# Rotary rotation of q and k by ScalarE copies between partition halves, instead of a TensorE product with a rotation matrix

## What is computed

```python
z = rms_norm_2(x, norm_g) @ w_in
aq, ak, av, ag, mq, mk, mv, mi, mf, mo, mgate = split(z)
q = rms_norm_2(aq.reshape(B, L, 16, 64), q_norm_g)     # a norm per token and head
k = rms_norm_2(ak.reshape(B, L, 2, 64), k_norm_g)
# rope on the first 16 of a head's 64 rows, in two halves of 8
x1, x2 = x[..., :8], x[..., 8:16]
x = concat([x1 * cos - x2 * sin, x2 * cos + x1 * sin, x[..., 16:]])
ya = sliding_window_sink_attention(q, k, v, sink)      # window 128, meta tokens always seen
```

## Time and profile before

| | |
|---|---|
| runs | 1529.10, 1522.83, 1528.91 us, median 1528.91 |
| the profiled execution's own time | 1525.94 us |
| its span | 1524.0 us |
| TensorE busy | 1480.7 us, 97% |
| VectorE busy | 1052.0 us, 69% |
| ScalarE busy | 765.5 us, 50% |
| GpSimd busy | 318.6 us, 21% |
| mean granted TensorE clock | 0.994 |

### The profile page before, as it was taken

The page is one execution under the profiler, slowest core; times in us unless marked ns, Lnnn a source line. Parts: engine busy times, 40 slices in busy tenths (PEclk is TensorE's granted clock), DMA queues, the critical chain, the costliest instruction groups (busy, mean ns, idle before and its releaser), DMA issues.

```text
span 1524.0 us, 31453 instructions
## 1 busy us (share of the span) xinstructions
PE 1480.7 (97%) x11939; PEld 1460.6 (96%) x11939; DVE 1052.0 (69%) x1999; ACT 765.5 (50%) x1270; POOL 318.6 (21%) x392
## 2 busy tenths in 40 slices
PE   7999998999999999999999999999999999999998
PEld 7999998899999999999999999889999999899898
DVE  6666578766655666557766656888678778876883
ACT  5454448555444554445554545446644453565442
POOL 4111113211101111014321114453320125231000
PEclk9999999999999999999999999999999999999999
DMA  6656754465555655554565555533343554334333
GB/s 207 186 179 200 241 166 139 152 189 184 181 174 185 186 184 181 173 188 154 162 192 180 179 176 157 152 107 116 91 119 107 164 145 123 99 98 125 111 117 120
DMA packets 245275, 239.65 MB, mean 157 GB/s; under 512 B 15160, under 2 KB 244392, under 8 KB 245048
## 3 DMA queue, kind: packets, MB, share of 16 engines
q1 hardware_dynamic: 245176, 238.29, 50.9%
HBM read 237.21 MB, written 1.05 MB: 156 GB/s over the span
## 4 chain that ended last, share of the span: by engine, by line
PE 84%; DVE 10%; ACT 2%; issue 2%; POOL 1%; DMA 0%; SPq 0%; DVEq 0%; ACTq 0%; POOLq 0%
PE bank L552 25%; PE bank L554 25%; PE bank L553 25%; DVE w_lo L1523 3%; PE bank L878 1%; PE bank L818 1%; PE bank L836 1%; ACT w_hi L967 1%; PE bank L801 1%; DVE work L1563 1%; DVE work L1680 1%; PE bank L884 1%; PE bank L894 1%; PE bank L817 1%; PE bank L837 0%
## 5 line engine op out<-in xcount | busy, mean ns | idle before, releaser
L1523 DVE TENSOR_TENSOR w_lo<-raw,w_hi 128x1024 fp32r<-128x1024 f32 (+1 forms) x456 | 563.0, 1244 | 303.8 <-ACT w_hi L967 303.5
L552 PE MATMUL bank<-x_hi,w_hi 128*128 128x256 f32 (+1 forms) x2480 | 719.0, 290 | 2.2 <-DVE w_lo L1523 2.2
L554 PE MATMUL bank<-x_hi,w_lo 128*128 128x256 f32 (+1 forms) x2480 | 707.1, 285 | 0.0
L553 PE MATMUL bank<-x_lo,w_hi 128*128 128x256 f32 (+1 forms) x2480 | 706.2, 285 | 0.0
L967 ACT CAST w_hi<-raw 128x1024 fp32r<-128x1024 f32 (+1 forms) x456 | 464.9, 1030 | 261.2 <-PE bank L554 250.1
L552 PEld LDWEIGHTS bank<-x_hi,w_hi 128*128 128x128 f32 x2480 | 476.0, 192 | 4.1 <-issue 2.0
L553 PEld LDWEIGHTS bank<-x_lo,w_hi 128*128 128x128 f32 x2480 | 476.1, 192 | 1.0
L554 PEld LDWEIGHTS bank<-x_hi,w_lo 128*128 128x128 f32 x2480 | 475.6, 192 | 0.0
L552 PE MATMUL bank<-y_hi,w_hi 128*128 128x256 f32 (+1 forms) x1088 | 310.2, 285 | 8.0 <-DVE y_lo L1534 8.0
L554 PE MATMUL bank<-y_hi,w_lo 128*128 128x256 f32 (+1 forms) x1088 | 309.5, 284 | 0.0
L553 PE MATMUL bank<-y_lo,w_hi 128*128 128x256 f32 (+1 forms) x1088 | 309.4, 284 | 0.0
(11 more groups left out here) (288 smaller groups left out, 1248.8 us busy)
## 6 DMA issues: line engine op xcount, KB each, us to landing
raw<-in_ffn_w_in_dram SPq DMA_DIRECT2D x176, 512.0 KB, 3.6
raw<-in_w_in_dram SPq DMA_DIRECT2D x100, 512.0 KB, 3.6
raw<-in_ffn_w_out_dram SPq DMA_DIRECT2D x64, 512.0 KB, 4.2
raw<-in_w_out_dram SPq DMA_DIRECT2D x32, 512.0 KB, 3.5
raw<-in_ffn_w_out_dram SPq DMA_DIRECT2D x32, 384.0 KB, 3.0
raw<-in_rec_w_in_dram SPq DMA_DIRECT2D x16, 512.0 KB, 3.7
raw<-in_sg_w_in_dram SPq DMA_DIRECT2D x16, 512.0 KB, 3.4
raw<-in_rec_w_out_dram SPq DMA_DIRECT2D x8, 512.0 KB, 3.4
```

The lines of the kernel that those rows point to most:

```text
L552: mm(acc, wh, xh, start=first and j == 0, stop=False)
L553: mm(acc, wh, xl, start=False, stop=False)
L554: i_ = mm(acc, wl, xh, start=False, stop=last and j == n - 1)
L1523: TT(w_lo[:, s, 0:n, :], raw[:, s, 0:n, :], w_hi[:, s, 0:n, :].bitcast(fp32), SUB).then_inc(lo_made, 1)
```

## The change

The rows of a head are laid out anew in q and k. The 64 rows of a head are taken as four blocks of 16; the first 8 rows of each block of both heads go to partitions 0 to 63, the last 8 to partitions 64 to 127 (head e of a chunk has partitions 32e to 32e+31 and 64+32e to 64+32e+31). So the two rows that a rotation mixes lie 64 partitions apart, and the rotation is a swap of partition halves and a signed sine.

- **Weights.** The order comes with the split of the weights: for the units of `kv` and `aq` `split_w` reads `raw` in runs of 8 columns and writes runs of 64, one instruction per half (three instructions for `kv`, whose v columns keep their order), on ScalarE and on VectorE.
- **Turn.** ScalarE copies the halves of `qs` crosswise into PSUM bank 5 or 6 (`swap_halves`, two copies of 64 x 272 per chunk) in place of TensorE's product; VectorE's add is a step `turned`, at the units where `turn` was. The means (`turn` on TensorE) are at u 5, 6, 8, 10, 12. ScalarE's square for k is taken at u 3.
- **rs, rt, kx** come one unit earlier: u 13, 14 and 15, 16. VectorE does `rs` before the tiles and the convolution of u 13.
- **Tail.** q's tail isn't normed: ScalarE copies it (eight copies of 32 x 64), the norm goes into the exponential's scale (`tail_r`), for which TensorE has one product of 18 columns and VectorE three small instructions. The eight `sel` products go.
- **k.** No swap product: ScalarE makes the crossed copies (four of 32 x 272), VectorE masks k by two multiplications of 128 x 272 in place of a copy and a memset.
- **Parameters.** The two norm gains are loaded by eight transfers, not four.

The pieces of the diff below are, in this order: the table of steps, the order of a head's columns, SyncE's transfers of the gains, TensorE's `turn`, `rt` and `kx`, ScalarE's `split_w` (VectorE's is alike), ScalarE's part of `turned`, and VectorE's `turned` and `rs`.

```diff
-    VISITS[5 if _c == 0 else 7 + 2 * ((_c - 1) // 2)].append(("turn", _c))
-VISITS[14].append(("rs", 0))
-VISITS[15].append(("rt", 0))
-VISITS[16].append(("rt", 1))
-VISITS[17].append(("kx", 0))
+    VISITS[5 if _c == 0 else 6 + 2 * ((_c - 1) // 2)].append(("turn", _c))
+    VISITS[5 if _c == 0 else 7 + 2 * ((_c - 1) // 2)].append(("turned", _c))
+RS_AT = 13
+VISITS[14].append(("rt", 0))
+VISITS[15].append(("rt", 1))
+VISITS[16].append(("kx", 0))
...
+        def half_of_heads(t, part, n, to=False):
+
+            if to:
+                return t[:, :, part * DH:part * DH + DH] if n == P else t.rearrange("p k (m c) -> p (k m) c", c=P)[
+                    :, :, part * DH:part * DH + DH]
+            if n == P:
+                return t[:, :, 0:P].rearrange("p k (b r i) -> p k r b i", r=2, i=8)[:, :, part]
+            return t.rearrange("p k (m b r i) -> p (k m) r b i", m=2, r=2, i=8)[:, :, part]
...
-                    for e in range(2):
-                        sp.dma_start(par_rows[r:r + k, t, e * DH:(e + 1) * DH], src).then_inc(par_loaded, 16)
+                    for part in range(2):
+                        for e in range(2):
+                            at = part * DH + e * QD
+                            sp.dma_start(par_rows[r:r + k, t, at:at + QD].rearrange("l (b i) -> l b i", i=8),
+                                         src.rearrange("l (b r i) -> l r b i", r=2, i=8)[:, part]).then_inc(par_loaded, 16)
...
-                        mm(bank[4][0:w, at:at + 2], score[:, n % 2, a:a + w], cst("head_mean"), start=True, stop=True)
-                    pe.wait_ge(qc_new, n + 1)
-                    pe.wait_ge(cos_ready, l + 1)
-                    if c >= 2:
-                        pe.wait_ge(q_ready, n - 1)
-                    mm(bank[5 + n % 2][:, 0:L], rot_g[:, 0 if c else 1, :], qs[:, n % 2, :], start=True,
-                       stop=True).then_inc(turn_mm, 1)
+                        i_ = mm(bank[4][0:w, at:at + 2], score[:, n % 2, a:a + w], cst("head_mean"), start=True, stop=True)
+                    i_.then_inc(turn_mm, 1)
...
-                        at = CONST_AT["sel"]
-                        mm(bank[6][:, 0:L], con[:, at:at + P], r_t, start=True, stop=True)
-                        for c in range(NC8):
-                            at = CONST_AT["sel"] + (c + 1) * P
-                            i_ = mm(bank[7][:, c * TAIL:(c + 1) * TAIL], con[:, at:at + P], r_t[:, 2 * P:L],
-                                    start=True, stop=True)
-                        i_.then_inc(rt_mm, 1)
+                        mm(bank[6][:, 0:L], cst("k_rows"), r_t, start=True, stop=True)
+                        mm(bank[7][:, 0:NR], cst("tail_rows"), norms[:, 3, 2 * NR:3 * NR], start=True,
+                           stop=True).then_inc(rt_mm, 1)
...
-                    pe.wait_ge(k_ready, l + 1)
-                    mm(bank[4][:, 0:L], cst("swap"), k_att, start=True, stop=True)
...
+                if isinstance(off, int) and U + off in ROWS_OF_HALVES:
+                    last = ROWS_OF_HALVES[U + off]
+                    for part in range(2):
+                        i_ = nc.scalar.copy(half_of_heads(w_hi[:, s, 0:n, :], part, last, True).rearrange(
+                            "p k (b i) -> p k b i", i=8), half_of_heads(raw[:, s, 0:n, :], part, last))
+                    if last < CU:
+                        i_ = nc.scalar.copy(w_hi[:, s, 0:n, last:CU], raw[:, s, 0:n, last:CU])
+                    i_.then_inc(hi_made, 1)
+                    return
...
+                def swap_halves(c):
+
+                    n = 9 * l + c
+                    act.wait_ge(qs_new, n + 1)
+                    if n >= 2:
+                        act.wait_ge(q_ready, n - 1)
+                    for part in range(2):
+                        dst, src = part * DH, DH - part * DH
+                        i_ = nc.scalar.copy(bank[5 + n % 2][dst:dst + DH, 0:L], qs[src:src + DH, n % 2, :])
+                    i_.then_inc(qs_swapped, 1)
...
-                    dve.wait_ge(turn_mm, n + 1)
+                    dve.wait_ge(qs_swapped, n + 1)
+                    dve.wait_ge(qc_new, n + 1)
                     TT(dst, bank[5 + n % 2][:, 0:L], qc[:, n % 2, :], ADD).then_inc(q_ready, 1)
...
+                            if u == RS_AT:
+                                rs()
                             if j == 1:
                                 tiles(ph, p, pr)
```

More of the change, by code:

```diff
@@ L24 @@
 M_MIN = -41.0
-WORK_SLOTS = 65
+WORK_SLOTS = 66
 AW = 3 * P
@@ L29 @@
 TAIL = 16
+QD = 32
 FULL = 80
@@ L36 @@
 C_AQ, C_KV, C_AG, C_MQK, C_MV, C_MIF, C_MO, C_MG = 0, 1024, 1280, 2304, 3328, 4352, 4360, 5384
-CONST_W = dict(ident=P, tri=P, amask=AW, tmask=L, mmask=P, rot=P, swap=P, head_mean=2, cos=L, sin=L, sel=(NC8 + 1) * P)
+CONST_W = dict(ident=P, tri=P, amask=AW, tmask=L, mmask=P, head_mean=2, cos=L, sin=L, k_rows=P, tail_rows=P, tail_head=ATT_H)
 CONST_AT = {}
@@ L61, in constants @@
     half = ROT // 2
-    for h0 in (0, DH):
-        for d in range(half):
-            c["rot"][h0 + half + d, h0 + d] = -1
-            c["rot"][h0 + d, h0 + half + d] = 1
-    c["swap"][i, (i + DH) % P] = 1
-    c["head_mean"][i, i // DH] = 1.0 / DH
+    c["head_mean"][i, i % DH // QD] = 1.0 / DH
+    c["k_rows"][i % DH // QD, i] = 1
+    c["tail_rows"][i % TAIL, i] = 1
     inv = (500000.0 ** (-np.arange(0, ROT, 2, dtype=np.float32) / ROT)).astype(np.float32)
@@ L70, in constants @@
     c["cos"][:] = 1
-    for h0 in (0, DH):
-        for k in (0, half):
-            c["cos"][h0 + k:h0 + k + half] = np.cos(ang)
-            c["sin"][h0 + k:h0 + k + half] = np.sin(ang)
-    for k in range(NC8 + 1):
-        for e in range(2):
-            c["sel"][2 * k + e, k * P + e * DH:k * P + (e + 1) * DH] = 1
+    for e in range(2):
+        for part, sign in ((0, 1), (1, -1)):
+            r = part * DH + e * QD
+            c["cos"][r:r + half] = np.cos(ang)
+            c["sin"][r:r + half] = sign * np.sin(ang)
+        for hd in range(e, ATT_H, 2):
+            r = e * DH + hd % 8 // 2 * TAIL
+            c["tail_head"][r:r + TAIL, hd] = 1
     return np.concatenate([c[n] for n in CONST_W], 1)
@@ L346, in build_stack @@
             sem(n) for n in ("ws_tr", "ws_read", "vt_tr", "vt_read", "sg_mm", "sg_read"))
[L348 to L349 removed]
+        cos_ready, qsq_new, qs_new, qs_swapped, qc_new, turn_mm, q_ready = (
+            sem(n) for n in ("cos_ready", "qsq_new", "qs_new", "qs_swapped", "qc_new", "turn_mm", "q_ready"))
         rs_new, rt_mm, rt_read, k_ready, tail_new = (
@@ L388, in build_stack @@
             cnt += k
+        ROWS_OF_HALVES = {U: P if ph == "kv" else CU for l in range(DEPTH) for ph in ("kv", "aq")
+                          for p in range(PHASES[f"{ph}{l}"][2]) for U, _, _ in PAIRS[PHASES[f"{ph}{l}"][1] + p]}
+        def half_of_heads(t, part, n, to=False):
[5 more added lines that the diff above has]
+            return t.rearrange("p k (m b r i) -> p (k m) r b i", m=2, r=2, i=8)[:, :, part]
         def units_of(pair):
@@ L1333, in _ @@
                                     later = (ph, p)
-                            for kind, n in [s for s in steps if s[0] != "turn"] + \
-                                    [s for s in VISITS[min(u + 1, STREAM_UNITS - 1)] if s[0] == "turn"]:
+                            for kind, n in steps:
                                 do[kind](n)
+                            for kind, n in [s for s in VISITS[min(u + 1, STREAM_UNITS - 1)] if s[0] == "turn" and s[1]]:
+                                turn(n)
                             u += 1
@@ L1522, in split_w @@
                 dve.wait_ge(hi_made, U + 1 + off)
+                if isinstance(off, int) and U + off in ROWS_OF_HALVES:
+                    last = ROWS_OF_HALVES[U + off]
+                    for part in range(2):
+                        lo, hi = (half_of_heads(t[:, s, 0:n, :], part, last, True).rearrange("p k (b i) -> p k b i", i=8)
+                                  for t in (w_lo, w_hi))
+                        i_ = TT(lo, half_of_heads(raw[:, s, 0:n, :], part, last), hi.bitcast(fp32), SUB)
+                    if last < CU:
+                        i_ = TT(w_lo[:, s, 0:n, last:CU], raw[:, s, 0:n, last:CU], w_hi[:, s, 0:n, last:CU].bitcast(fp32), SUB)
+                    i_.then_inc(lo_made, 1)
+                    return
                 TT(w_lo[:, s, 0:n, :], raw[:, s, 0:n, :], w_hi[:, s, 0:n, :].bitcast(fp32), SUB).then_inc(lo_made, 1)
```

79 lines of the change are left out of this document (46 added, 33 removed).

## The result

The changed kernel takes **1533.07 us** (median of 8 runs, 1532.24 to 1533.83) against 1525.37 for the kernel before (8 runs beside it): ratio 1.0046, 95% interval 1.0035 to 1.0057. The forecast was 1521.0 with a range up to 1532. The time lies 12 us above the forecast and 1 us outside the range, on the slower side.

What follows compares the result with a forecast made beforehand. TensorE, busy in 97% of the span, was taken to bound the kernel. From 1525.94 us, 9.5 gained at the first scores was subtracted and 4.6 of clock loss added: 1521.0 us, forecast 1517 to 1525, overall range 1510 to 1532.

Steps and rivals of the forecast that it cites:

- TensorE's removed work: Both layers: eighteen rotation products (9.9 us), the `sel` products and k's swap go, 13.8 us of TensorE's time together.
- TensorE's arrival at `rt`: TensorE reaches `rt`, now behind u 14, at 998.3 in layer 0 and about 1284 in layer 1.
- VectorE's arrival: Rotation's last add, which `rt` waits for, ends at 1005.9 and 1291.9, with `rs` adding 4.35 us and cut splits 0.5.
- the very coupling that a rival had hoped would loosen: VectorE's splits slowed beside GpSimd; apart, 2.4 us back per layer; with clock held 1511.6, with one about 1516.3; chance 0.28.
- The waits at `rt`: TensorE waits at `rt` for VectorE some 7.6 us in layer 0 and 8 us in layer 1.
- The clock: Behind the waits at `rt` TensorE's clock falls to 1.2 GHz, costing 2.3 us in each layer, 4.6 in all.
- From `rt` to the first scores: TensorE's stretch from `rt` to the first scores takes 14.4 us, where it took 14.18 before.
- the gain at the first scores: First scores come 3.0 us earlier in layer 0 and 6.5 in layer 1, 9.5 us taken as gain before clock loss.
- The rival "nothing is gained": TensorE waits again at the first scores or for a split, 1 to 3 us per layer: 1526 us; chance 0.13.
- "Short runs are slow": Reading `raw` in 32-byte runs at half rate costs 1.04 us more per split: 1535.6 us; chance 0.09.

Runs made afterwards that it cites:

- the third experiment: Changed kernel with each weight split in one piece again on both engines, without the new row order (other output): 1529.49 us.
- the fourth experiment: Changed kernel with 14 unused float32 products per layer keeping TensorE busy ahead of the waits of `rt`: 1528.22 us.
- the fifteenth experiment: Changed kernel with GpSimd's product `qc` done twice in a row: 1542.69 us.
- the tenth: Changed kernel, `rt` transposes in bank 7, two ScalarE splits ahead of waiting work, k's masks and copies of v and gate rows on ScalarE: 1525.71 us.
- the first: Changed kernel with the transposes of `rt` in free bank 7, the wait for the rotation's last add moved to the spreading products: 1526.28 us.
- fifth: Changed kernel with the convolution's second tap left out of the computation: 1524.65 us.
- seventh: Changed kernel, `rt` transposes in bank 7, VectorE's tables, k masks and copies of v and gate rows given to ScalarE: 1528.00 us.
- the sixth experiment: Changed kernel, `rt` transposes in bank 7, rotation's last two adds and ScalarE's copies for them ahead of u 13's tiles and convolution: 1525.06 us.

## Why the prediction was wrong

- **TensorE's removed work** (13.8 us): the products are gone, but 0.55 us was too much for one. Two sums of means with two rotation products took 1.89 us (990.64 to 992.53), the two sums alone take 1.10 (978.33 to 979.43): 0.40 for a rotation product, 7.2 us for the eighteen and not 9.9, and about 11 us in all. Busy time fell by only 5.6 us, because the granted clock took back most of the rest. Besides the places named below it was 0.78 over 7.6 us from 970.7 and 0.76 over 7.3 us from 1271.3. So the clock cost TensorE some 10.6 us in five places (an estimate: 1.7 in each of these two, 1.6 and 2.5 behind `rt`, 3.1 behind the third head's scores), against 4.65 in the two places of the earlier trace rows before.
- **TensorE's arrival at `rt`**: 998.3 forecast; it was 1008.76 - 8.04 = 1000.7. The stream began 0.5 later, the waits for squares were 1.3 us as estimated, and the clock fell to 0.64 from 972 to 976, behind the first of them, 1.4 us that I hadn't counted. In layer 1 the waits for squares were 2.0. The four pairs of sums took 4.4 and not 4.0.
- **VectorE's arrival**: the last add forecast at 1005.9, measured at 1008.5. VectorE began 0.6 later and took 42.5 us where 40.55 were forecast. Its idle time was 1.6 us, about the 1.4 that I had left in. `rs` took 4.9, not 4.35, and line 1932 1.04, where the same instruction took 0.42 before. The ten splits took 16.0 us in the timeline, against 14.2 before, where I had added 0.5. The answer to the earlier trace rows, with 2.49, 2.82, 1.64 and 1.55 for the same six units before:

```profile
966.00 2.50 DVE L1572 TENSOR_TENSOR w_lo<-raw,w_hi 128x512 fp32r<-128x512 f32 x4 [1.52 <-ACT w_hi L976]
973.50 3.63 DVE L1572 TENSOR_TENSOR w_lo<-raw,w_hi 128x512 fp32r<-128x512 f32 x4
980.30 2.38 DVE L1572 TENSOR_TENSOR w_lo<-raw,w_hi 128x512 fp32r<-128x512 f32 x2
982.60 1.79 DVE L1577 TENSOR_TENSOR w_lo<-raw,w_hi 128x1024 fp32r<-128x1024 f32 x1
```

  By the third experiment five cut units are 0.75 of the 1.8 us. For the rest I have only the theory that the splits lie beside GpSimd's products more than before, the very coupling that a rival had hoped would loosen; no run shows its share.
- **The waits at `rt`** (7.6 and 8): 8.04 and 7.21, near in layer 0 by luck: both engines came some 2.5 us later than forecast, and the two errors cancel in the wait.
- **The clock** (2.3 in each): 1.6 and 2.5 by the fourth experiment, 4.1 in place of 4.6: right.
- **From `rt` to the first scores** (14.4): without the clock 14.21. So 70.37 us from the start in layer 0 against 69.6 + (-3.0 + 2.3) = 68.9 forecast: 1.5 over, the same 1.5 in layer 1.
- **The step that failed** is that I stopped there. The sum takes the gain at the first scores for the kernel's gain. In the rivals I even counted VectorE's work between `rt` and the scores (10.5 us in 12.5) as an argument that it would be on time. But in the kernel before it was exactly on time three units later, at the third head's scores, after a stretch in which it was busy 88% of the time. Its maximum (line 1947) ended at 1034.93, and TensorE began the product at 1034.98, without a wait:

```profile
1034.47 0.46 DVE L1947 TENSOR_SCALAR work<-work,neg_sinks 128x1 f32<-128x1 f32 x2
1034.98 0.49 PE L817 MATMUL bank<-work 128*128 128x128 f32 x2
```

  The change gave that stretch 3.9 us more of VectorE's work. So the gain at the first scores was spent three heads on: +3.16 and -0.25 us where I had -0.7 and -4.2. One of the two waits there also lost the clock, 3.1 us. The whole miss of the profiled execution, 11.6 us, adds up so: 1.5 twice up to the first scores, 2.4 twice from there to the third head's (14.1 us in each layer, where it was 11.7), 3.1 of clock, and 0.7 ahead of the streams and at the end.
- **The rival "nothing is gained"** had the mechanism, waits of 1 to 3 us per layer for VectorE, placed at the first scores, and priced it at 1526 with a chance of 0.13. It missed the clock behind the new wait, and that VectorE's queue also grew. "Short runs are slow" has fallen: the cut costs 0.15 to 0.17 us per unit, not 1.04, and less than the 0.35 from which it decides. Still the cut alone turned out to be half the loss, by the waits and the clock behind it.

## What to carry to other kernels

When TensorE stands at 97% but its waits are for one engine, follow that engine's queue past the edit, to the last place where it was just on time, and make the sum there. Here about 11 us taken off TensorE were worth nothing, because that queue set the time. A better order took back what the change had lost (7 us by one wait moved), but no order brought a complete kernel clearly under the old time: past that point moving instructions only chose where TensorE waited. So count busy and idle time of the queue in the stretch, before and after. An engine that is half idle isn't free: what is moved to it delayed what stood behind it (ScalarE's splits), and more work on GpSimd slowed VectorE.

## What the runs showed of the hardware

- VectorE and GpSimd slow each other on operands in SBUF: in the fifteenth experiment an instruction of 0.22 us takes 0.66 to 0.80 beside a GpSimd product of 0.75. In the changed kernel a product of GpSimd that takes 0.77 us elsewhere took 3.11 beside two splits (996.66). Nine more products per layer cost 4 us each layer at `rt`.
- The clock falls behind waits of one length in one execution and not in another: a wait of 1.82 to 1.84 us at the third head's scores of layer 0 cost 1.5 or 3.1 us of clock in all six profiled executions that have it. In layer 1 it cost nothing in three (the changed kernel, the third and fourth experiments) and 1.5 and 3.1 us in two (the tenth and fifteenth). Waits of 0.5 to 0.8 us at the same place of layer 0 cost nothing (the first, fifth and seventh).
- In the sixth experiment the time of an execution went with its mean granted clock: eight executions took 1524.3 to 1525.5 us at 0.989 to 0.991, and three took 1530.4 to 1531.8 at 0.984 to 0.987.
- Cutting the splits in two, with reads of the weights in runs of 32 bytes, costs 0.15 to 0.17 us a unit in all (the third experiment). Half the rate in reading them would have cost 1.04 us a unit by the prediction's sum, so it isn't that.
